# Output projection: block 2 prepared ahead of the loop, its transfers issued earlier, and the first blocks' softmax sums spread by TensorE

## The reference

```python
# yr_l: RWKV scan, 6 heads of 64;  ya_l: grouped attention, 6 heads;  yn_l: neighbourhood attention, 4 heads
y_l = jnp.concatenate([yr_l * jax.nn.silu(rg_l), ya_l * jax.nn.silu(ag_l),
                       yn_l * jax.nn.silu(ng_l)], axis=-1) @ w_out
x = _layer_norm(DEEPNORM_ALPHA * x + gate[:, None] * y_l, ln_g, ln_b)
```

## Time and profile before

| | |
|---|---|
| median of 3 runs | 4583.74 us (4580.54 to 4589.02) |
| profiled execution | 4589.19 us, span 4587.1 us |
| mean granted TensorE clock | 0.936 |
| PE busy | 3955.6 us, 86% |
| DVE, POOL, ACT busy | 2697.1, 1584.8, 1534.8 us |
| moved by DMA | 572.35 MB, 125 GB/s over the span |

### The profile page before, as it was taken

The page is one execution under the profiler, slowest core; times in us unless marked ns, Lnnn a source line. Parts: engine busy times, 40 slices in busy tenths (PEclk is TensorE's granted clock), DMA queues, the critical chain, the costliest instruction groups (busy, mean ns, idle before and its releaser), DMA issues. The chain is left out here.

```text
span 4587.1 us, 105292 instructions
## 1 busy us (share of the span) xinstructions
PE 3955.6 (86%) x44004; PEld 3093.9 (67%) x44004; DVE 2697.1 (59%) x4502; ACT 1534.8 (33%) x2727; POOL 1584.8 (35%) x1276
## 2 busy tenths in 40 slices
PE   6999788877998699978885998689878888987888
PEld 4878688845666587758884676578635667863566
DVE  3466355555666547545555665765576656557665
ACT  1233233324552123323332653210155621014562
POOL 2233144412015423314442112665242255533225
PEclk8999999988998899989997999889989989998999
DMA  5445533352236454552324244533412464341246
GB/s 190 161 170 187 172 89 85 85 205 53 61 90 202 144 162 174 204 168 74 82 72 156 48 99 132 185 99 111 143 49 61 115 179 129 110 138 56 62 103 185
DMA packets 572613, 572.35 MB, mean 125 GB/s; under 512 B 150728, under 2 KB 470364, under 8 KB 570132
## 3 DMA queue, kind: packets, MB, share of 16 engines
q1 hardware_dynamic: 444628, 488.21, 35.3%
q10 hardware_dynamic: 127616, 78.95, 6.0%
HBM read 378.80 MB, written 192.42 MB: 125 GB/s over the span
## 5 line engine op out<-in xcount | busy, mean ns | idle before, releaser
L1096 PE MATMUL pr_acc<-hH,pr_wh 128*128 128x512 f32 (+1 forms) x1288 | 481.7, 374 | 0.0
L1097 PE MATMUL pr_acc<-hL,pr_wh 128*128 128x512 f32 (+1 forms) x1288 | 465.2, 361 | 0.0
L1098 PE MATMUL pr_acc<-hH,pr_wl 128*128 128x512 f32 (+1 forms) x1288 | 465.1, 361 | 0.0
L2753 ACT ACTIVATE an_p<-an_p,an_stat 128x1280 f32<-128x1280 f32 (+5 forms) x372 | 339.9, 915 | 138.6 <-DVE an_stat L2810 134.9
L2706 PE MATMUL an_t<-ident,an_p 128*128 128x128 f32 x2152 | 313.0, 281 | 36.4 <-ACT an_pT L2760 23.5
L2487 POOL TENSOR_TENSOR an_kl<-mo_w,an_kh 128x1280 fp32r<-128x1280 f32 (+3 forms) x36 | 79.3, 2202 | 758.1 <-DVE an_qh L2477 757.9
L2806 DVE CUSTOM_DVE_ANT_0 an_p<-an_s,an_mask 128x256 f32<-128x256 f32 (+8 forms) x308 | 275.1, 893 | 103.4 <-PE an_s L2689 67.1
L1465 POOL TENSOR_TENSOR sp_sl<-sp_w,sp_sh 128x512 fp32r<-128x512 f32 x172 | 246.0, 1437 | 195.7 <-DVE sp_sh L1540 177.3
L2706 PEld LDWEIGHTS an_t<-ident,an_p 128*128 128x128 f32 x2152 | 236.6, 141 | 110.5 <-ACT an_pT L2760 46.2
L1140 POOL TENSOR_TENSOR pr_wl<-pr_w,pr_wh 128x1024 fp32r<-128x1024 f32 x58 | 143.1, 2468 | 469.9 <-DVE pr_wh L1160 469.9
L2004 DVE TENSOR_TENSOR rk_tu<-rk_tu,rk_ps 128x512 f32<-128x512 f32 x300 | 189.0, 683 | 196.3 <-PE rk_ps L1828 196.2
(11 more groups left out here) (378 smaller groups left out, 9746.1 us busy)
## 6 DMA issues: line engine op xcount, KB each, us to landing
CHK<-ri_out SPq DMA_DIRECT2D x24, 1920.0 KB, 7.9
rk_in<-CHK SPq DMA_DIRECT2D x240, 128.0 KB, 2.5
pr_w<-in_w_in ACTq DMA_DIRECT2D x58, 512.0 KB, 4.3
UT<-pr_out SPq DMA_DIRECT2D x45, 640.0 KB, 4.6
sp_w<-in_w_in ACTq DMA_DIRECT2D x50, 512.0 KB, 5.2
U<-sp_c SPq DMA_DIRECT2D x100, 256.0 KB, 2.0
mod_w<-in_w_mod SPq DMA_DIRECT2D x16, 1024.0 KB, 7.9
mo_w<-in_w_out SPq DMA_DIRECT2D x16, 1024.0 KB, 8.3
```

The lines of the kernel that those rows point to most:

```text
L1096: nc.tensor.matmul(out, wh[:, u, k, 0:m], hi, start=(k == 0), stop=False)
L1097: nc.tensor.matmul(out, wh[:, u, k, 0:m], lo, start=False, stop=False)
L1098: ins = nc.tensor.matmul(out, wl[:, u, k, 0:m], hi, start=False, stop=(k == KT - 1))
L2753: nc.scalar.activation(row, row, ACT.Exp, bias=stat[:, n % NPM, j, 1:2], scale=heads[groups[n][0]].scale, accum_out=total[:, sum_column(n, ...
```

## The change

1. **Sums of the first two blocks.** The reciprocals stay in SBUF behind attention. For blocks 0 and 1 DVE copies each head's column 64 times (`wide`), TensorE turns these 128x128 pieces (5 a block in block one, 6 in block two) into PSUM, and DVE multiplies the gate by the result (`gate_normed`). The four RCP transfers of these blocks, POOL's `divided(0)` and `divided(1)` and the four small matmuls are gone. `lower_ready` goes from POOL to DVE.
2. **Weights.** Chunks 0, 1 and 2 are loaded in attention, at groups NG-6, NG-5 and NG-3; only chunk 3 is behind it.
3. **Three blocks ahead.** Block 2 is prepared before the loop, between the work on chunk 2 and on chunk 3; in the loop the block prepared is t + 3 and not t + 2, and ACT's norm(t) goes ahead of upper(t + 3).
4. **SP.** load(2) is issued ahead of the loop; in the loop load(t + 1) comes before the row of x of block t and its wait.
5. **Two more releases,** one behind each RWKV output in `block_one`.

```diff
-                    if kind == "store" and x in (NG - 4, NG - 3):
+                    if kind == "store" and x in (NG - 6, NG - 5, NG - 3):
                         sp.wait_ge(lo.sem, lo.nth(len(heads)))
                         sp.wait_ge(au.sem, au.nth(aug_no[-1]))
-                        inputs.weights.load(sp, x - NG + 4)
+                        if x == NG - 3:
+                            sp.wait_ge(vt.sem, vt.nth(vturns_to(len(kvs) - 1)))
+                        inputs.weights.load(sp, (NG - 6, NG - 5, NG - 3).index(x))
...
-                    sums_of(t, late_in[t].sem)
...
-                for i in range(2, weights.CHUNKS):
-                    weights.load(sp, i)
+                weights.load(sp, 3)
                 row(0)
                 row(1)
                 for i, v in enumerate(vectors):
                     sp.dma_start(vecs[:, i, :], v.to_broadcast([P, DM])).then_inc(cst.sem, 16)
+                load(2)
                 for t in range(2, nblk):
-                    load(t)
+                    load(t + 1)
+                    sp.wait_ge(z_ok.sem, z_ok.nth(t - 1))
+                    row(t)
...
                 rounded(2, 1)
+                tanh(2)
                 rounded(3, 0)
+                upper(2)
                 rounded(3, 1)
                 for t in range(nblk):
-                    if t + 2 < nblk:
-                        tanh(t + 2)
-                        upper(t + 2)
+                    if t + NY < nblk:
+                        tanh(t + NY)
                     norm(t)
+                    if t + NY < nblk:
+                        upper(t + NY)
...
-                lower_ready(0)
-                lower_ready(1)
-                divided(0)
                 lower_later(0)
-                divided(1)
                 lower_later(1)
+                divided(2)
+                lower(2)
...
-                warm(core, ps[:, 3072:3328], 4)
+                for t in range(2):
+                    pe.wait_ge(wd.sem, wd.nth(t + 1))
+                    for i in range(nsum):
+                        two = wide[:, t, 2 * i:2 * i + 2, :].rearrange("p h d -> p (h d)")
+                        ins = nc.tensor.transpose(spread(t)[:, i * P:(i + 1) * P], two, core.ident[:])
+                    ins.then_inc(bc.sem, 1)
                 first_two()
...
+                def gate_normed(t):
+
+                    dve.wait_ge(bc.sem, bc.nth(t + 1))
+                    for i in range(len(later)):
+                        rows, sums = summed_part(i)
+                        spread_i = spread(t)[:, sums.start * P:sums.stop * P].rearrange("p (k t) -> p k t", t=P)
+                        ins = V.tensor_tensor(gt[:, t, rows], gt[:, t, rows], spread_i, ALU.mult)
+                    ins.then_inc(gn.sem, 1)
+                    dve.wait_ge(gn.sem, gn.nth(t + 1))
...
+                for t in range(2):
+                    V.tensor_copy(wide[:, t], heads_rcp[:, :, t:t + 1].to_broadcast([P, 2 * nsum, HD])).then_inc(wd.sem, 1)
...
-                for i in (2, 3):
-                    for j in range(2):
-                        split(i, j)
+                split(2, 0)
+                split(2, 1)
+                gated(2)
+                split(3, 0)
+                split(3, 1)
...
         rwkv_core(core)
         rwkv_output(core, l)
+        core.release()
```

More of the change, by code:

```diff
@@ L2400, in __init__ @@
         self.OT = core.sb(s, "an_oT", [P, NOUT, 2 * P])
-        self.rcpT = core.sb(s, "an_rcpT", [sums, P])
+        self.rcp, self.rcpT = core.sb(s, "an_rcp", [P, sums]), core.sb(s, "an_rcpT", [sums, P])
         self.loaded = [core.move(f"mo_w_loaded{c}") for c in range(self.CHUNKS)]
@@ L2557, in attention @@
         rank = [sum(other.row < head.row for other in heads) for head in heads]
-        total, rcp = core.sb(s, "an_sum", [P, NT]), core.sb(s, "an_rcp", [P, NT])
+        total, rcp = core.sb(s, "an_sum", [P, NT]), inputs.weights.rcp
         mask = core.sb(s, "an_mask", [P, TT + P])
@@ L2873, in mixed_out @@
     ready_in = [core.move(f"mo_ready_in{t}") for t in range(2)]
-    late_in = [core.move(f"mo_late_in{t}", len(later) + 2) for t in range(2)]
+    late_in = [core.move(f"mo_late_in{t}", len(later)) for t in range(2)]
     y_in, x_in, yg_in = core.landing("mo_y_loaded", per=3 + len(gates)), core.landing("mo_x_loaded"), core.landing("mo_yg_loaded")
@@ L2902, in mixed_out, with spread @@
         first = slice(*ready)
+        wide = core.sb(s, "mo_wide_sums", [P, 2, 2 * nsum, HD])
+        heads_rcp = weights.rcp[:].rearrange("p (h t) -> p h t", h=2 * nsum)
+        def spread(t):
+            return ps[:, (2 + t) * 1024:(2 + t) * 1024 + nsum * P]
         def summed_part(i):
@@ L2937, in load @@
                 def load(t):
+                    if t >= nblk:
+                        return
                     u = t % 2
@@ L2946, in load @@
                         grown(t, yg_in.on(u))
-                    sp.wait_ge(z_ok.sem, z_ok.nth(t - 1))
-                    row(t)
                 for t in range(2):
@@ L3056, in divided @@
                     u = t % 2
[L3057 to L3060, removed]
+                    pool.wait_ge(y_in.on(u), y_in.step(t - 2, u))
                     for i in range(len(later)):
@@ L3155, in opened, with lower_ready @@
                     dve.wait_ge(gm.sem, gm.nth(t + 1))
+                def lower_ready(t):
+                    dve.wait_ge(yr_hi.sem, yr_hi.nth(t + 1))
+                    V.tensor_tensor(YL[:, t, first], YT[:, t, first], YH[:, t, first], ALU.subtract).then_inc(yr_lo.sem, 1)
+                def gate_normed(t):
[6 more added lines that the diff above has]
+                    dve.wait_ge(gn.sem, gn.nth(t + 1))
                 def gated_ready(t):
@@ L3161, in gated_later @@
                 def gated_later(t):
-                    dve.wait_ge(yn.sem, yn.nth(t + 1))
+                    dve.wait_ge(late_in[t].sem, late_in[t].after(1))
                     for i, (a, b) in enumerate(later):
@@ L3211, in split @@
                     V.tensor_tensor(WL[:, 2 * c + j, :], W[:, c, j], WH[:, 2 * c + j, :], ALU.subtract).then_inc(w_lo.sem, 1)
+                for t in range(2):
+                    V.tensor_copy(wide[:, t], heads_rcp[:, :, t:t + 1].to_broadcast([P, 2 * nsum, HD])).then_inc(wd.sem, 1)
                 split(0, 0)
-                split(0, 1)
                 if ncm:
+                    lower_ready(0)
+                    split(0, 1)
+                    lower_ready(1)
+                    opened(0)
+                    gate_normed(0)
                     split(1, 0)
-                    opened(0)
                     gated_later(0)
+                    opened(1)
+                    gate_normed(1)
                     split(1, 1)
-                    opened(1)
                     gated_later(1)
                 else:
+                    split(0, 1)
                     opened(0)
                     gated_ready(0)
+                    gate_normed(0)
+                    lower_ready(0)
                     opened(1)
                     gated_ready(1)
+                    gate_normed(1)
+                    lower_ready(1)
+                    gated_later(0)
                     split(1, 0)
-                    gated_later(0)
                     split(1, 1)
                     gated_later(1)
-                for i in (2, 3):
-                    for j in range(2):
-                        split(i, j)
+                split(2, 0)
[3 more added lines that the diff above has]
+                split(3, 1)
                 dve.wait_ge(cst.sem, cst.after(1))
```

23 lines of the change are left out of this document (11 added, 12 removed).

## The result

| | median, us | runs |
|---|---|---|
| before | 4586.38 | 4580.54 to 4595.59, 4 runs |
| after | 4557.24 | 4551.49 to 4563.33, 4 runs |

The ratio is 0.9936 with a 95% interval of 0.9921 to 0.9951: 29 us faster, between 22 and 36 of 4584. Forecast were 22.4 us and 4561, range 4537 to 4580. The profiled execution took 4551.49 us, its span is 4549.7 (before 4587.1); TensorE's mean granted clock is 0.939 for 0.936.

What follows compares the result with a forecast made beforehand. Late block 2 data, behind full DMA engines, hold TensorE at each stage's start, with low clock after. Four stages save 25.4 us, releases cost 3.0: 22.4 less, 4583.7 to 4561.3, predicted 4561, range 4537 to 4580.

Steps and rivals of the forecast that it cites:

- Step 1, the arrival: Start of each stage: fewer bytes ahead bring block 2's data sooner, 2.5 us by chunk 2, 2.7 or 3.3 by sums.
- Step 2, chunk 3 queued behind the data: Chunk 3's splitting waits behind block 2's preparation; block 2's products start at A + 14.9, in block two A + 16.1.
- A: Time when block 2's data land in each stage, forecast as 1406.0, 2836.2, 3681.2 and 4488.4 us.
- Step 3, nothing waits after block 2: Later blocks on TensorE: the 0.44 us holes go, each block takes 10.93 us; stages 6.8, 5.9, 6.9, 5.8 us shorter.
- What follows the last matmul stays: End of each stage: the time behind TensorE's last matmul was taken as unchanged.
- DVE and POOL still hold the loop: Rival, chance 0.07: the shared port keeps blocks at 11.59 us, losing 4.6 + 3.3 us in the first two stages; 4569.
- Step 4, the additions at nothing: Before the first products: copies, multiplications and transposes, 5 to 9 us of DVE, counted as 0; without cover up to 3 a stage.
- Step 5, the releases: Behind the RWKV outputs in block one: two added releases cost 1.5 us each, 3.0 us in all.
- no earlier: Rival, chance 0.14: issue on SP holds block 2's data, so they come no sooner; 4583, no change.
- slower: Rival, chance 0.09: load(2) waits on DVE's additions, A comes 3 us after today's; 4595.
- The stall is smaller: Rival, chance 0.22: at chunk 3, data 4 us sooner give 16 us, matmuls that stay warm some 6; 4539.
- A hole under 3 us: Sign against the forecast: TensorE's hole before block 0's chunk 3 products, expected about 6 us, under 3 means a smaller stall.

Runs made afterwards that it cites:

- u2: Changed kernel with the early chunk undone: weight chunks 0 and 1 loaded in attention, 2 and 3 behind it; ratio to before 0.9968.
- u1: Changed kernel with the first two blocks' reciprocal sums again by four transfers and POOL, four warm matmuls for the transposes; ratio to before 0.9985.
- u4: Changed kernel with block 2's tanh, product and cast put behind chunk 3's rounding and splitting on ACT and DVE; ratio to before 0.9892.
- u12: Changed kernel with chunk 3 split first, vectors loaded behind block 2's loads, and POOL's shift on one column in all blocks but the last; ratio to before 0.9882.
- u9: Kernel before with the two added releases alone; ratio to before 1.0009, interval 0.9998 to 1.0021.
- u10: Changed kernel with 6 small matmuls on TensorE between chunk 2's and chunk 3's products, filling the wait for block 2's data; ratio to before 0.9900.

## Why the prediction was right, and where not

*Step 1, the arrival.* Counted from attention's end, block 2's tanh moved from 32.3, 31.0, 33.7 and 32.2 us to 27.2, 24.1, 26.8 and 26.4: 5.2, 6.9, 6.9 and 5.8 sooner, 24.7 together, against 5.2, 5.2, 5.8 and 5.8, 22.1. u2 and u1 give the parts: 1 MB is worth 2.2 us (2.5 forecast), the sums 3.5 in block one and 5.1 in block two (2.7 and 3.3). The four transfers of sums cost more than their bytes at the mixed rate that I took; 0.79 MB in 5.1 us would be 154 GB/s, but 1.5 to 2.6 us of it is load(2) being issued later (u1), so that is no rate of the small rows.

*Step 2, chunk 3 queued behind the data.* This came as forecast: the first splitting's products at A + 4.41 (4.45), in 2.90 us (2.7), the second's at A + 7.79 (8.1). From A to the stage's end I had 102.5, 80.7, 81.9 and 81.9 us; measured are 100.1, 80.4, 78.7 and 80.3. Block 2's products start at A + 12.6, 14.9, 13.3 and 14.9 where I had 14.9, 14.9, 16.1 and 16.1. In stages 3 and 4 I carried the pattern of stage 1 over, but there the holes were only 1.1 to 1.8 us, and the first matmul behind them shows 0.50 us, not 0.8: the clock was still up. In stage 4 it fell 1.0 us later, for 3.4 us (the row at 4468.89 shows 0.63); in stage 3 it stayed up. I named this wait as a step and priced it inside the sum; I did not price its absence. u4 shows that it was worth 20 us, two thirds of what the whole change had brought. "The trace lacks some records" was a wrong reading: all 480 and 384 matmuls of a stage are there, and a block takes 10.88 us and not 10.93, some 1 us over the four stages.

*Step 3, nothing waits after block 2.* For TensorE it is right. "What follows the last matmul stays" is the sentence that failed: the tails grew by 5.0 and 2.5 us. The loop of the sums ran at 11.3 us a block against TensorE's 10.9, hidden until the end by the four product buffers and three operands ahead. The rival "DVE and POOL still hold the loop" had the engines right, u12 shows it, and the place wrong: not TensorE's holes but the tail.

*Step 4, the additions at nothing.* The products of the four stages start 5.0, 5.8, 12.0 and 10.7 us behind attention's end, before 5.6, 6.5, 11.0 and 11.4; the two copies take 0.45 us each. All additions together are 3.7 us of DVE in block one and 3.9 in block two, under the 5 to 9 that I had, and TensorE's waits for the lower parts of blocks 0 and 1 are 17.6 us (L3169 and L3080 above) where the kernel before had 59.1 - 29.7 = 29.4.

*Step 5, the releases.* 3.0 against 4 (-1 to 10) by u9's ratio, which leaves the size open. The traces say that 1.5 us each was too much. Behind the RWKV output no engine computed for 1.95 and 2.61 us in the kernel before already, which has a barrier there; with the release it is 2.91 and 3.10, 1.45 us more in all. And the clearings behind stages 1 and 2 are 0.46 and 0.37 us shorter with it. That leaves 0.6 us for the two, and 0.3 by the same count in u9.

*The sum.* 35.7 from the products, less 7.5 in the tails and 0.6 for the releases, is 28; the ratio says 29, between 22 and 36. The two profiled executions themselves lie 37.4 us apart. The other 10 us are in stretches that the change doesn't touch, 9 of them between the release behind stage 1 and the end of attention in stage 2: 1282.7 us before, 1273.3 after. That stretch takes 1272.6 to 1282.1 us in the twelve kernels with the change or a variant of it and 1283.9 in u9: it differs by as much from execution to execution, but both kernels without the change lie above all twelve, and no run isolates whether a part of it belongs to the change. So my 22.4, at the lower edge of what was measured, came that near by errors against each other, which is luck: the products were 10.3 us better (2.6 by the arrival, 7.4 by what follows it in steps 2 and 3), the releases 2.4 cheaper, and the tails 7.5 worse. Of the other rivals, "no earlier" and "slower" fell with the first row of ACT. "The stall is smaller" held in stages 2 to 4, whose holes at chunk 3 add up to 3.5, 2.0 and 2.9 us, not in the first with 7.0. A hole under 3 us I had named as a sign that the forecast is wrong; stages 3 and 4 show it, and stage 2 stands at the border. The time came out between the forecast's 4561 and that rival's 4539, near the forecast.

## What to carry to other kernels

When an engine prepares later work ahead of work that is ready, ask whether the later work's data are there: in an in-order queue a wait for data belongs behind everything that doesn't need them, and here the two lines in the wrong order cost 20 us. Price a hole on TensorE with the low clock behind it, which can be more than the hole (here 4.8 us behind 3.5). Read a loop's period on every engine: an engine slower than the bound one by 0.4 us a block is hidden by buffers, and comes out behind the last block.

## What the runs showed that I had not expected

A release took part of the next one's work over: the clearing behind stage 1 was 871 ns in the kernel before and 416 ns in the kernel after. In the third row below, from u9, which is the kernel before with the added releases alone, it is 395, so it is the release ahead of it that shortens it, itself 503 ns in both:

```profile
L184 POOLq EVENT_SEMAPHORE_RANGE_CLEAR  x1: 503/503/503, 1036.6 to 1036.6; - x1
L184 POOLq EVENT_SEMAPHORE_RANGE_CLEAR  x1: 416/416/416, 1525.5 to 1525.5; - x1
...
L184 POOLq EVENT_SEMAPHORE_RANGE_CLEAR  x1: 395/395/395, 1528.4 to 1528.4; - x1
```

Of the same operation on DVE, the addition of x, one loop shows 2.19 us and another 1.23; POOL's shift, which stands beside it in the first, is itself 3.37 us there and 2.34 at its shortest. Left open are how much of u10's gain is the clock, and whether bytes or SP's issue set the arrival of block 2's data.
